# Neighbourhood attention: probabilities turned by a matmul with a diagonal of reciprocal sums

## What is computed

```python
s_lat = einsum('bnqhd,bknshd->bhnqks', qb, k_s) * scale + bias      # masked outside the window
s_ctx = einsum('bnqhd,bchd->bhnqc', qb, kc) * scale
p = softmax(concatenate([s_lat, s_ctx], axis=-1), axis=-1)
o = einsum('bhnqks,bknshd->bnqhd', p_lat, v_s) + einsum('bhnqc,bchd->bnqhd', p_ctx, vc)
# context queries
p = softmax(einsum('bqhd,bkhd->bhqk', q_c, k_c) * scale); o_c = einsum('bhqk,bkhd->bqhd', p, v_c)
```

## Time and profile before

| | |
|---|---|
| median of 3 runs | 3070.98 us |
| lowest and highest | 3070.7 and 3072.57 us |
| the profiled execution's own time | 3072.22 us |
| its span | 3069.8 us |
| attention stage, first scores to the next stage's first transpose | 878.2 to 968.8 us |

### The profile page before, as it was taken

The page is one execution under the profiler, slowest core; times in us unless marked ns, Lnnn a source line. Parts: engine busy times, 40 slices in busy tenths (PEclk is TensorE's granted clock), DMA queues, the critical chain, the costliest instruction groups (busy, mean ns, idle before and its releaser), DMA issues.

```text
span 3069.8 us, 40707 instructions
## 1 busy us (share of the span) xinstructions
PE 2860.1 (93%) x15782; PEld 2658.3 (87%) x15782; DVE 1474.5 (48%) x1848; ACT 1094.9 (36%) x1465; POOL 646.5 (21%) x336
## 2 busy tenths in 40 slices
PE   5899999989977797999999899999998987899999
PEld 5899999978965687999999899999997855668887
DVE  7874366254556836652564422222225557543332
ACT  3342144125455333431342243112212657454221
POOL 4441144120013714430342300000022113110000
PEclk8999999999999898999999999999999989899999
DMA  6443144111210012441342112211211210123233
GB/s 259 155 147 124 57 158 151 63 43 52 72 38 1 1 42 103 157 154 58 130 157 93 37 62 62 75 55 61 72 51 56 62 55 1 42 75 101 91 96 103
DMA packets 67666, 258.70 MB, mean 84 GB/s; under 512 B 7424, under 2 KB 8576, under 8 KB 66944
## 3 DMA queue, kind: packets, MB, share of 16 engines
q1 hardware_dynamic: 50016, 192.58, 18.9%
q10 hardware_dynamic: 17568, 65.02, 6.0%
HBM read 255.47 MB, written 2.10 MB: 84 GB/s over the span
## 4 chain that ended last, share of the span: by engine, by line
PE 81%; DVE 10%; ACT 2%; issue 2%; POOL 1%; DMA 0%; DVEq 0%; ACTq 0%; POOLq 0%
PE G L428 20%; PE G L432 20%; PE G L430 20%; PE G L435 5%; PE G L439 5%; PE G L437 5%; DVE tmp L1433 2%; DVE B L1304 1%; DVE xl L1422 1%; DVE sL L1632 1%; PE NP L691 1%; PE G L782 1%; DVE wl L1299 1%; DVE sL L1623 1%; PE NP L600 1%
## 5 line engine op out<-in xcount | busy, mean ns | idle before, releaser
L890 ACT ACTIVATE wh<-raw 128x1024 fp32r<-128x1024 f32 (+1 forms) x300 | 338.8, 1129 | 1578.0 <-PE G L432 1285.0
L428 PE MATMUL G<-xh,wh 128*128 128x384 f32 x2752 | 711.3, 339 | 73.4 <-DVE xl L1422 47.7
L430 PE MATMUL G<-xl,wh 128*128 128x384 f32 x2752 | 704.7, 337 | 0.0
L432 PE MATMUL G<-xh,wl 128*128 128x384 f32 x2752 | 704.0, 336 | 0.0
L1299 DVE TENSOR_TENSOR wl<-raw,wh 128x1024 fp32r<-128x1024 f32 (+1 forms) x300 | 429.4, 1431 | 406.8 <-ACT wh L890 406.0
L428 PEld LDWEIGHTS G<-xh,wh 128*128 128x128 f32 x2752 | 500.3, 190 | 87.6 <-issue 40.9
L430 PEld LDWEIGHTS G<-xl,wh 128*128 128x128 f32 x2752 | 503.0, 190 | 0.0
L432 PEld LDWEIGHTS G<-xh,wl 128*128 128x128 f32 x2752 | 501.9, 190 | 0.0
L1910 POOL TENSOR_TENSOR mraw<-mraw,scb 128x1024 f32<-128x1024 f32 x120 | 315.0, 2625 | 598.7 <-DVE B L1304 598.7
L428 PE MATMUL G<-hh,wh 128*128 128x384 f32 x1056 | 268.0, 334 | 0.0
L432 PE MATMUL G<-hh,wl 128*128 128x384 f32 x1056 | 267.8, 334 | 0.0
(11 more groups left out here) (308 smaller groups left out, 3104.3 us busy)
## 6 DMA issues: line engine op xcount, KB each, us to landing
raw<-in_w SPq DMA_DIRECT2D x176, 512.0 KB, 3.6
mraw<-in_wmn ACTq DMA_DIRECT2D x120, 512.0 KB, 4.4
raw<-in_w SPq DMA_DIRECT2D x64, 704.0 KB, 4.1
raw<-in_abin SPq DMA_DIRECT2D x24, 512.0 KB, 3.5
raw<-in_cdin SPq DMA_DIRECT2D x20, 512.0 KB, 3.6
mini<-in_wmn SPq DMA_DIRECT2D x9, 512.0 KB, 14.8
gmini<-in_wmn SPq DMA_DIRECT2D x2, 2048.0 KB, 22.0
raw<-in_about SPq DMA_DIRECT2D x8, 512.0 KB, 3.6
```

The costliest lines, as they stand in the source:

```text
L428: pe.matmul(bank(h), W, tokens(rh, h), start=(k == 0), stop=False)
L430: pe.matmul(bank(h), W, tokens(rl, h), start=False, stop=False)
L432: mm = pe.matmul(bank(h), L, tokens(rh, h), start=False, stop=(k == nk - 1))
L890: act.activation(wh[slot][:, 0:nk * P], raw[slot][:, 0:nk * P], ACT.Copy).then_inc(hi_done, 1)
```

## The change

`normalise` no longer multiplies nsP. It makes a tile ndiag (one for even and one for odd units, 128 x 256 each): the identity matrix, 128 x 128, times the reciprocal sum of each row, for a context unit two such blocks with the two columns of sums. Since ndiag(u) is read by turn(u), `normalise(u)` waits for turn(u-2). `turn` multiplies each block of the unnormalised nsP by the diagonal, in place of a transpose with the identity; a product of nsP's block with a diagonal on the other side is the transpose with each query's column scaled.

```diff
+        ndiag = [at(f"ndiag{s}", [P, 2 * P], SQ + 2304 + 2 * P * s) for s in range(2)]
...
                     for c in range(4):
-                        mm = pe.transpose(G[1][:, 512 * (u % 2) + P * c:512 * (u % 2) + P * c + P],
-                                          nsP[u % 2][:, P * c:P * c + P], cst("ident"))
+                        w_ = 0 if u < 32 else c // 2
+                        mm = pe.matmul(G[1][:, 512 * (u % 2) + P * c:512 * (u % 2) + P * c + P],
+                                       nsP[u % 2][:, P * c:P * c + P], ndiag[u % 2][:, P * w_:P * w_ + P], start=True, stop=True)
...
+                    if u >= 2:
+                        dve.wait_ge(tr_done, u - 1)
                     for w_ in range(nw):
-                        r = slice(0, 512) if nw == 1 else slice(256 * w_, 256 * w_ + 256)
-                        ins = dve.tensor_scalar(nsP[u % 2][:, r], nsP[u % 2][:, r], st[:, 4 + w_:5 + w_], None, ALU.mult)
+                        ins = dve.tensor_scalar(ndiag[u % 2][:, P * w_:P * w_ + P], cst("ident"), st[:, 4 + w_:5 + w_], None,
+                                                ALU.mult)
                     ins.then_inc(pn_ready, 1)
```

## The result

The changed kernel takes 3077.59 us, the median of 14 runs (3073.23 to 3080.0), beside 3071.41 us of the kernel before in 14 runs (3067.05 to 3074.38). The ratio is 1.002, with a 95% interval of 1.0012 to 1.0028: some 6 us or 0.2% slower. The profiled execution has a span of 3073.4 us, 3.6 us more than that of before; why this is less than the medians say comes further down. The page of the changed kernel, against the earlier trace rows: TensorE has 160 instructions and 14.7 us of work more (the turns alone add 40 x 0.5 = 20 us; why the total grew by less comes further down, too).

The account below looks back on a forecast made before the run. TensorE, 93% busy, was taken as the bound, through the attention pairs' chain over multiply and odd turn. Terms 4.3 + 0.3 + 0.43 + 2 x 0.37 + 0.9 gave +6.7 us: 3077.7, range 3074.0 to 3080.8.

Parts of the forecast that it names:

- Latent pairs: Attention pairs 1 to 14: odd turn 0.505 us longer, held multiply 0.197 us shorter, together +4.3 us.
- Tail by width: VectorE's multiply in latent pairs: time behind GpSimd's end goes with width, 0.28 us for 512 columns, 0.085 for 128.
- Added wait: normalise(u) on VectorE now also waits for turn(u-2); always met when reached, so 0.
- Pair 15: Attention pair whose multiply is no longer held: turn +0.505, multiply -0.20, so +0.3 us.
- pair 16: Chain goes over ScalarE; the longer even turn delays exp, copy and the second exp: +0.43 us.
- pairs 17 and 18: Context pairs: multiply ends 0.135 us earlier, odd turn ends 0.505 later, +0.37 us each.
- The end: Last turns of the attention stage: the even turn loses cover and turn 39 waits for TensorE, +0.9 us.
- the small multiply that is not held: Rival, latent pairs: the 128-wide instruction escapes GpSimd's hold and takes 0.285 us; +0.6 us, 3071.6; chance 0.12.
- The fixed tail: Rival, latent pairs: 0.28 us behind GpSimd's end at any width; +9.5 us, 3080.5; chance 0.09.
- the cheaper product: Rival, turns: the first step also takes 0.112 us, each turn 0.1 cheaper; +4.7 us, 3075.7; chance 0.09.
- the fourfold one: Rival, turns: a plain product costs four transposes, +1.27 us for each turn; +23 us, 3094; chance 0.02.

Follow-up runs that it names:

- The two parts alone: Turns as plain products with the identity in the kernel before: 3081.92 us; changed kernel with transposes again, diagonals made but unread: 3068.51 us.
- the wider diagonal: Changed kernel with the latent units' diagonal instruction 256 instead of 128 columns wide, second half never read: 3079.61 us in one run.
- the kernel with the late tile: Changed kernel with GpSimd's bias tile of unit u also waiting for normalise(u-3), so it starts behind the diagonal's instruction: 3071.87 us, ratio 1.0004.

## Why the prediction was right

The forecast was 3077.7 us and +6.7 us; the medians give 3077.59 and +6.2, in the range of 3074.0 to 3080.8. Its steps:

- *Latent pairs, +0.308 us each.* Right: 4.86 or 4.87 us instead of 4.56 or 4.57, so +0.30. The turn came out at 1.16 us and the diagonal at 0.72, both as worked out from the earlier trace rows. The two parts alone gave 5.06 and 4.37 us a pair, +0.50 and -0.20.
- *Tail by width.* Right: 0.08 us for 128; the wider diagonal confirms 0.15 for 256.
- *Added wait, 0.* Right in the pairs that set the time.
- *Pair 15, +0.3; pair 16, +0.43; pairs 17 and 18, +0.37 each.* Right: by the starts of the context scores the stage had shifted by 4.48 us at scores(16), where 4.6 was forecast, then by 0.43, 0.36 and 0.37 more. In pair 16 the second exp starts at 956.17, directly behind copy, and the odd turn had ended at 955.92, so it was the even turn that counted, as forecast.
- *The end, +0.9.* Too much: +0.73. The step that was off is the start of turn 39, taken as a turn of its own behind turn 38. Turns 38 and 39 now run through without a break (16 records in 2.09 us): turn 39 starts 0.11 us behind the last record of turn 38, so 0.3 later than before and not 0.4, and its second record comes 0.15 us behind its first, not 0.215.

A context pair of the changed kernel, which answers to the earlier trace rows (timeline):

```profile
958.31 1.16 PE L585 MATMUL G<-ndiag,nsP 128*128 128x128 f32 x8
...
959.57 0.47 ACT L1067 ACTIVATE nsP<-G,nst 128x256 f32<-128x256 f32 x1 [1.72 <-PE G L585]
...
959.75 1.16 PE L585 MATMUL G<-ndiag,nsP 128*128 128x128 f32 x8 [0.28 <-DVE ndiag L1570]
...
961.00 0.47 ACT L1067 ACTIVATE nsP<-G,nst 128x256 f32<-128x256 f32 x1
```

The even turn (958.31) ends at 959.47 and exp starts 0.10 later; the second exp follows copy and the odd turn. This is the delay by the even turn that the prediction took for pair 16.

The sum of the stage was +6.4 us (90.65 to 97.0 us) where 6.7 was forecast, so the forecast is right by its terms. That the absolute time agrees to 0.1 us is in part luck: the kernel before came out 0.4 us above the median of 3 runs that the forecast started from, and the rise 0.5 us below. Of the rivals, the small multiply that is not held has the right price (the kernel with the late tile: 0.286 us, 4.43 us a pair, and the time of the kernel before), but its condition did not come: GpSimd stayed ahead by 0.03 us. The fixed tail, the cheaper product and the fourfold one fell.

**The profiled executions differ by less than the stage.** The stage cost 6.4 us there, the whole span 3.6. The difference lies behind it, mostly in the SSD part, whose code is the same. The rows of its stretch (us, busy of PE, PEld, DVE, ACT, POOL, granted clock, DMA), first before, then after:

```profile
991.00:1081.00 90.00, 63.84 (x570) 58.69 (x569) 70.19 (x171) 28.19 (x50) 59.41 (x53) 0.85 0.00 1
```

```profile
997.60:1085.00 87.40, 58.35 (x569) 53.63 (x568) 70.95 (x171) 27.49 (x49) 60.81 (x54) 0.94 0.00 1
```

The clock granted to TensorE was 0.85 of full speed in the one and 0.94 in the other, that is, more time at 1.2 GHz in the one than in the other. TensorE was busy for 5.5 us less there with the same work, which is why its total grew by 14.7 us and not by 20. The part from the stage's end to the first product of the norm at the end of the SSD took 111.8 and 109.8 us. In the profiled executions of the other kernels, with the same code there, it took between 109.9 and 113.0 us, with no relation to the edit. The runs of each kernel spread over 7 us as well. So I take it for scatter from one execution to the next; what decides it was not settled. The prediction put it down to the shift of the later stretches, and that no run shows. The medians of 14 runs, +6.2 us, agree with the stage, not with the two profiled spans.

## What to carry to other kernels

Before making an instruction narrower, look at whether its length goes with its width: here 0.44 of 0.93 us was a wait for GpSimd inside the instruction, which shows only as an end at the same distance behind the other engine's end each time, and one wait on the idle engine removed it. Price both halves of a trade on the chain that repeats: 0.2 us off VectorE and 0.5 us onto TensorE stand one behind the other in each pair. And ask first why a step stands in the chain where it does; the order of two steps on VectorE was worth 15 us, more than the two parts of the change moved (+10.3 and -3.2), and it made a kernel in which TensorE's added work costs still more. A chain that names one engine can run beside a loop without slack on two others: look at what the engine's instructions are released by.

## What the runs showed of the hardware

- A fp32 tensor_scalar from SBUF to SBUF that starts 0.03 us behind a GpSimd tensor_tensor ends 0.08, 0.15 or 0.28 us behind its end, for 128, 256 or 512 columns; alone it takes 0.286, 0.353 and 0.487 us. With its source in PSUM the 128-wide one takes 0.35 and is not held.
- A plain fp32 product of 128 x 128 by 128 takes two records, 0.112 us apart, a transpose one. The second record of a turn comes after 0.215 us where the turn follows a wait or the scores, and after 0.11 to 0.15 where it follows another turn without a break. Four transposes take 0.66 us and four products 1.16; eight without a break take 1.09 and 2.05 to 2.09.
- With the order changed, most of the hold vanished without an edit to GpSimd (0.49 and 0.60 us instead of 0.93), since its tiles then ran beside a maximum that reads PSUM or while VectorE waited.
